# Where a 12-buffer weight ring changes to 4 MB transfers: three pairs of experts written out instead of five

## What is computed

```python
def moe_ffn(h, w_router, b_router, w1, b1, w2, b2):
    ...
    top_val, top_idx = lax.top_k(logits, TOP_K)
    ...
    for e in range(N_EXPERTS):
        u = t @ w1[e] + b1[e]
        glu = jnp.minimum(u[:, :D_EXPERT], SWIGLU_LIMIT)
        lin = jnp.clip(u[:, D_EXPERT:], -SWIGLU_LIMIT, SWIGLU_LIMIT)
        a = glu * jax.nn.sigmoid(SWIGLU_ALPHA * glu) * (lin + 1.0)
        out = out + gates[:, e:e + 1] * (a @ w2[e] + b2[e])
```

## Time and profile before

| | us |
|---|---|
| median of 3 executions | 1123.87 (1122.37 to 1125.55) |
| the profiled execution, its own time | 1125.64 |
| span of the profiled execution, first to last instruction | 1123.2 |
| PE busy in it | 1080.0 |
| VectorE (DVE) busy | 333.9 |
| ScalarE (ACT) busy | 196.0 |
| DMA traffic | 438.65 MB, mean 391 GB/s |

### The profile page before, as it was taken

How to read it: one execution, slowest core, us unless ns; L and a number is a source line. 1 busy time by engine, 2 the same in 40 slices (tenths; PEclk the granted TensorE clock), 3 DMA queues, 4 the chain that set the end, 5 groups by cost and what they waited for, 6 DMA issues and landing times.

```text
span 1123.2 us, 12635 instructions
## 1 busy us (share of the span) xinstructions
PE 1080.0 (96%) x5174; PEld 507.7 (45%) x5174; DVE 333.9 (30%) x609; ACT 196.0 (17%) x335; POOL 36.7 (3%) x45
## 2 busy tenths in 40 slices
PE   9999999999999999999999898989898989898997
PEld 8887878734343443434343333324242424242432
DVE  4887767323121221212122112112121203021212
ACT  7676575400000000100000000000000000000000
POOL 1007120000000000000000000000000000000000
PEclk9999999899999999999999999999999999999999
DMA  9763349899999999999999999999999999999996
GB/s 361 292 201 136 128 146 425 364 377 427 429 427 427 428 427 428 433 434 432 429 430 432 431 431 431 436 433 431 431 432 431 431 433 434 433 431 431 424 425 283
DMA packets 27412, 438.65 MB, mean 391 GB/s; under 512 B 3185, under 2 KB 3441, under 8 KB 6513
## 3 DMA queue, kind: packets, MB, share of 16 engines
q1 hardware_dynamic: 26496, 431.46, 91.2%
q10 hardware_dynamic: 880, 6.69, 1.5%
HBM read 437.08 MB, written 1.05 MB: 390 GB/s over the span
## 4 chain that ended last, share of the span: by engine, by line
PE 72%; DMA 24%; DVE 3%; ACT 1%; issue 0%; POOL 0%; SPq 0%; POOLq 0%; DVEq 0%; ACTq 0%
DMA ring<-in_expert_q 24%; PE bank L905 22%; PE bank L930 20%; PE bank L498 11%; PE bank L873 5%; PE bank L836 5%; PE bank L485 3%; PE bank L776 2%; DVE ring_s L1387 1%; PE bank L764 1%; PE bank L549 1%; PE bank L598 0%; DVE gate_r L1418 0%; PE bank L871 0%; PE bank L623 0%
## 5 line engine op out<-in xcount | busy, mean ns | idle before, releaser
L905 PE MATMUL bank<-ring,feat_r 128*64 128x512 f32 x1504 | 337.4, 602 | 13.5 <-DMA ring<-in_expert_q 13.5
L905 PEld LDWEIGHTS bank<-ring,feat_r 128*64 128x64 f32 x1504 | 105.5, 138 | 235.3 <-issue 211.3
L930 PE MATMUL bank<-ring,feat_r 128*64 128x512 f32 x768 | 173.3, 596 | 9.6 <-DMA ring<-in_expert_q 9.1
L1667 DVE TENSOR_SCALAR late_r<-bank 128x512 f32<-128x512 f32 x32 | 22.1, 692 | 425.3 <-PE bank L905 425.3
L498 PE MATMUL bank<-ring_s,feat_s 128*128 128x512 f32 (+2 forms) x440 | 133.9, 385 | 0.2 <-issue 0.2
L905 PE MATMUL bank<-pool_r,feat_r 128*64 128x512 f32 x512 | 118.5, 610 | 10.5 <-DMA pool_r<-in_expert_q 10.5
L930 PEld LDWEIGHTS bank<-ring,feat_r 128*64 128x64 f32 x768 | 53.1, 137 | 116.4 <-issue 103.7
L1284 ACT ACTIVATE late_r<-late_r 128x512 f32<-128x512 f32 x32 | 20.2, 630 | 469.5 <-DVE late_r L1667 469.5
L1691 DVE TENSOR_TENSOR acc_r<-bank,acc_r 128x512 f32<-128x512 f32 x64 | 44.3, 692 | 151.8 <-PE bank L873 151.8
L498 PEld LDWEIGHTS bank<-ring_s,feat_s 128*128 128x128 f32 x440 | 78.7, 188 | 13.8 <-issue 2.0
L498 PE MATMUL bank<-ring_s 128*128 128x512 f32 (+2 forms) x216 | 81.2, 376 | 0.0
(11 more groups left out here) (202 smaller groups left out, 664.3 us busy)
## 6 DMA issues: line engine op xcount, KB each, us to landing
ring<-in_expert_q SPq DMA_DIRECT2D x45, 4096.0 KB, 27.5
ring<-in_expert_q SPq DMA_DIRECT2D x44, 2048.0 KB, 20.3
pool_r<-in_expert_q SPq DMA_DIRECT2D x15, 4096.0 KB, 29.1
pool_r<-in_expert_q SPq DMA_DIRECT2D x16, 2048.0 KB, 20.6
ring<-in_head_w SPq DMA_DIRECT2D x23, 1024.0 KB, 4.9
ring<-in_expert_q SPq DMA_DIRECT2D x15, 1024.0 KB, 10.2
ring<-in_head_w SPq DMA_DIRECT2D x6, 768.0 KB, 10.9
qkT_r<-in_expert_q ACTq DMA_DIRECT2D x1, 2048.0 KB, 12.1
```

The costliest lines, as they stand in the source:

```text
L905: mm = pe.matmul(b[e * SLOTS:(e + 1) * SLOTS, :], xT[:, k, e * SLOTS:(e + 1) * SLOTS], w[:, e, g, :], start=(late and k == 0), stop=(k == ...
L930: mm = pe.matmul(bank[4 + h][e * SLOTS:(e + 1) * SLOTS, :], aT[k // 4][:, k % 4, e * SLOTS:(e + 1) * SLOTS], w[:, q, e, :], start=(k == 0) ...
L1667: ts(glu, bank[2 * f][:], LIMIT, None, ALU.min).then_inc(sem(f"glu_ready{f}"), 1)
```

## The change

Two constants change. The loop of two pairs each now runs six times instead of five.

```diff
-ONCE = (33, 42, 51)
-FRONT_PAIRS = 5
+ONCE = (23, 25, 27)
+FRONT_PAIRS = 3
```

## The result

The changed kernel takes 1128.12 us (median of 7 executions, 1127.70 to 1129.36), the kernel before 1123.20 us in the same series (7 executions). The ratio is 1.0046, 95% interval 1.0037 to 1.0056: slower by 5.2 us (4.2 to 6.3). The forecast was +5.0 us and 1128.9.

What follows compares the result with a forecast made beforehand. The sum of all DMA transfers was taken to set the end. Gaps of 6.7 us less 0.8 for rate gave +5.9, landings +4.7; +5.0 taken on 1123.87 made 1128.9 us, range 1125.8 to 1131.6.

Steps and rivals of the forecast that it cites:

- The bound: Whole kernel: the sum of DMA transfers sets the end; queue idle time behind 240 us comes back whole, front PE work is free.
- The rate: Pairs 3 and 4: 12 transfers of 4 MB in place of 24 of 2 MB save 0.8 us (0.3 to 1.3).
- The triggers: Pairs 2 and 3: 4 MB transfers issue only after two parts are read; bias delays some by 2.4 or 4.6 us.
- quads A, C, D and E: Successive 4 MB two-part transfers from pair 3 on (A: parts 36, 37); forecast gaps 3.0, none, 1.3 and 2.4 us.
- The price of a start from empty: At each gap: a transfer issued to an empty queue costs 2.3 us beside its bytes, from a 1 MB landing.
- The sum: Whole kernel: gaps less rate give +5.9 us, summing by landings +4.7; +5.0 taken.
- The halves: Three gaps, 6.7 us: about half from used-once parts with the two-part wait, half from the moved bias.
- the upper bound: Restart after a gap also runs slowly at first, as at 230 to 240 us, adding 0.9 us: +6.8.
- Gaps that cost little: Rival: at the gaps, the next transfer starts under the tail of the last; +2.4 to +3.4 us, chance 0.17.
- the queue never runs empty: Rival: no gaps in the DMA queue, only the better rate left, -0.8 us, 1123.1; chance 0.04.
- A price per transfer: Rival: each of 12 transfers removed by merging gives back 2.3 us, 27.6 in all, about 1103; chance 0.01.
- More than the gaps: Rival: PE waits in pair 3 or 4, issues later, and gaps feed on themselves; +7 to +10 us, chance 0.08.

Runs made afterwards that it cites:

- e2: Kernel before with only the second bias added in pair 2 instead of pair 4; ratio 1.0002 to the kernel before, +0.2 us.
- e7: Kernel before with seven pairs written out instead of five, so 24 more 2 MB transfers replace 12 of 4 MB, bias in pair 6; ratio 1.0009, +1.0 us.
- e8: Kernel before with used-once parts 33, 42, 43 and 12 transfers of 4 MB for 24 from part 34 on; 1122.42 us against 1123.32, ratio 0.9987.
- e4: Changed kernel with the second bias back in pair 4; ratio 1.0036 to the kernel before, +4.0 us.
- e3: Kernel before with used-once parts 23, 25, 27 and the bias in pair 2, still 2 MB transfers in pairs 3 and 4; ratio 1.0044, +4.9 us.
- e6: As e4, but used-once buffers hold parts 13, 18, 23 instead of 23, 25, 27; ratio 1.0037 to the kernel before, +4.2 us.
- e1: Kernel before with only the used-once buffers holding parts 23, 25, 27 instead of 33, 42, 51; ratio 1.0012, +1.3 us.
- e5: As e4, but parts 36 and 37 come as two 2 MB transfers, each fetched when its slot is free; ratio 1.0025 to the kernel before, +2.8 us.

## Why the prediction was right, step by step

**The bound.** Right. The lost time stands in the DMA queue between 346 and 398 us, PE is busy all through it, and the loss comes back as PE waits in the loop. e2 shows that PE work in the front is free as long as the queue has work.

**The rate.** 0.8 us (0.3 to 1.3) was to be saved by 12 transfers in place of 24. e7 undoes such a saving and measured +1.0 us (0 to 2.0); e8 makes one and measured -1.5 us (-2.5 to -0.4). Both intervals hold the 0.8.

**The triggers.** Right within 0.5 us. Shifted by the 2.2 us of the head, quads A, C, D and E were issued at 353.8, 373.0, 384.2 and 396.3; forecast were 353.5, 372.5, 383.9 and 396.0. That the bias delays D by part and E by all of its 4.64 us is confirmed by e4 (2.5 and 4.6 us sooner).

**The price of a start from empty.** This term was sized too small. 2.3 us came from the landing of a 1 MB transfer, and e3's 2 MB transfer has 7.2 - 4.9 = 2.3 too. But a landing shows only a part of what a start costs, and the rest comes out at a later landing: in the trace of the kernel before, the two landings behind that of the earlier trace rows are 3.6 and 3.0 us apart, where a full queue has 2.5, and the prediction did not use them. The whole price is the time lost in bytes, less the time from the landing of the transfer ahead to the issue (negative where the issue came first):

| started | lost, by windows | issue after the landing ahead | price |
|---|---|---|---|
| quad A, changed kernel, 4 MB | 4.8 | 1.0 | 3.8 |
| quad D, changed kernel, 4 MB | 1.1 | -2.6 | 3.7 |
| quad E, changed kernel, 4 MB | 2.3 | -1.1 | 3.4 |
| part 44, e3, 2 MB | 2.5 | -1.2 | 3.7 |
| part 32, e6, 2 MB | 4.9 | 1.3 | 3.6 |

The landings ahead were at 350.6, 384.6 (quad C, issued at 370.8, 13.9 later), 395.2, 392.6 and 331.8. So the price is 3.4 to 3.8 us, and about the same for 2 and for 4 MB. Quad C, issued 4.2 us before quad B landed (359.2 + 15.8 = 375.0), lost nothing. Quad A shows what it is made of. In its 4.8 us, 2.3 are lost before the transfer ahead has landed, while some engines have already run dry (250 GB/s from 346 to 350, nothing from 350 to 350.6); 1.0 passes until the issue at 351.6; 0.9 from there to the first packets at 352.5; and 0.6 goes in the 5.5 us after that, which move 381 GB/s. The slow first microseconds that the upper bound had taken from the earlier trace rows are real, then, but they are the smallest part. Put into the prediction's own working, 3.6 in place of 2.3 makes the first gap 353.5 + 3.6 - 352.8 = 4.3 and leaves the others, which hang on the gaps before them, at 1.3 and 2.4: 8.0 in all. Forecast were 3.0 + 1.3 + 2.4 = 6.7; measured are 4.9 + 0.9 + 2.5 = 8.3.

**The sum.** That it came out right is in part luck. The gaps of 8.3 us less the 0.8 of the rate would make 7.5. The kernel before had itself lost 1.1 us at three late landings (5.1, 5.7 and 5.0 us apart instead of 4.9) in the stretch up to part 59, so the changed kernel was 475.5 + 2.2 = 477.7 against 471.4, 6.3 behind, where the way of summing by landings had put it 4.7 behind. From part 61 to the last landing it was then 0.9 us quicker (632.7 us against 633.6), since the profiled execution of the kernel before had more such late landings there. The profile has 5.4 us at the last landing, the ratio 5.2. Such single late landings, of 0.2 to 1.5 us each, come in every trace here, with a full queue too; they differ from run to run, and neither way could have them. So 4.7 and the 1.6 that the price was short make the 6.3; 0.9 of it came back by chance, and 0.3 had been added in choosing 5.0 between the two sums.

**The halves.** The text gave half of the gaps to the used-once parts with the two-part wait and half to the bias. As shares these are not well defined. Alone, the parts cost 1.3 us (e1), the bias 0.2 (e2); together 4.9 (e3); the parts with the 4 MB transfers 4.0 (e4); all three 5.2. The costs do not add up, since each of them only lengthens or shortens a time for which the queue may have work left. How much of the 5.2 goes with the bias alone, 1.2 by ratios or 2.8 by landings, stays open.

**The rivals.** "Gaps that cost little" wanted +2.4 to +3.4 us, and the interval begins at 4.2; "the queue never runs empty" is refuted by the window of 350.5 to 352.5. A price per transfer is refuted by e7. "More than the gaps" did not come: PE waits for weights from pair 5 on, when three quads are under way at a time.

## What to carry to other kernels

When transfers set the end and the compute engine runs ahead of them at first, look at how much work lies in the queue at each issue (time to landing less its own length), not at the engine's waits. In these runs a transfer had to be issued about 3.6 us before the one ahead of it landed, or the difference was lost. A buffer that is used once lends the queue one transfer of stock until it is read: let it hold a part that is read after the coarse, two-part waits have begun, so that the stock is there when they need it. Such costs come by thresholds: two edits that cost 1.3 and 0.2 us alone cost 4.9 together, and mending the first gap moved most of it (e5).

## What was not expected of the hardware

The price of an empty queue does not stand at the landing that follows it. The first transfer behind the gap shows 2.3 to 3.9 us beside its own length, and the rest comes out one to four landings later (quad F here, part 38 in e1, part 48 in e3, quad A in e6), when the queue is full again. Who reads landings alone sees gaps that aren't there and thinks small transfers cheaper to start than large ones; the windows put the loss where it arose, and there 2 MB and 4 MB cost about the same. Why the landings are shared out so was not tried.

Also, the queue drains unevenly: in the 4 us before 350 the DMA engines were busy for 0.59 of the time, and the last bytes of part 35 landed at 350.6, so some of the 16 engines had nothing to do up to 2 us before the landing. An issue that comes just before a landing is thus already too late. The window 346 to 410 holds all three gaps and lost (428 - 377) / 428 x 64 = 7.6 us of throughput in the changed kernel, the 8.3 less the better rate:

```profile
346.00:410.00 64.00, 64.00 (x300) 24.84 (x298) 11.32 (x21) 3.58 (x7) 0.00 (x0) 1.00 0.91 377
```
